# A transformer and two mixing blocks on one core: the second blocks' stages in another order

## The chip, the cores and the metric

The kernel runs on one core of a Trainium2 chip. The metric is the device time of one execution in microseconds (us). Runs are compared by their median.

## The reference, cut to what matters

The input has 256 latent and 256 context tokens of width 1024. Two transformer layers with attention and feed-forward parts come first; the change does not touch them. Then come two "second blocks" on the 256 latent tokens, and the change is in their first part, the mixer:

```python
def second_block(x, ...):
    for l in range(2):
        h = rms_norm(x, g_mix[l])
        aq, ak, av, iq, ik, iw, glu_in, cc_in, sb_in, gate_in = split(h @ w_in[l])
        # qa, ka, qi, ki: norms and rotary products of aq, ak, iq, ik
        y_a = dsa_attention(qa, ka, va, qi, ki, iw) @ w_oa[l]     # 4 heads of 128, the 64 best keys of a query
        u = causal_dwconv(glu_a * sigmoid(glu_b), cb_conv_w[l], cb_conv_b[l])     # 31 taps, 512 channels
        y_b = silu(layer_norm(u, ...)) @ w_ob[l]
        y_c = (gb * causal_dwconv(gc * xc, cc_conv_w[l])) @ w_oc[l]               # 3 taps
        y_d = stick_breaking_attention(sq, sk, sv) @ w_od[l]                      # 4 heads of 128
        gates = sigmoid(gate_in + b_gate[l])                                     # 4 x 1024
        merged = gates[0]*y_a + gates[1]*y_b + gates[2]*y_c + gates[3]*y_d
        x = x + merged @ w_merge[l]
        # feed-forward part with a convolution of 3 taps, unchanged
```

## The kernel before, in words

All matrix products are fp32 products made of three: every weight w is split into w_hi (ACT casts it, `split` at L1219) and w_lo = w - w_hi (DVE subtracts, `split` at L1713), every activation likewise, and `products` (L713) multiplies hi by hi, lo by hi and hi by lo. Weights come in **units** (`Run`, `Unit`, L165 to L185): 256 columns by eight blocks of 128 rows, 1 MB, 48 matmuls of 256 columns on PE. The units of w_oa to w_od have four row blocks, half of all that; ik and iw are smaller still. SP loads unit n when unit n-4 is done. `split_ahead(u)` (L1230, L1723) splits the unit two behind u, so each stage of ACT and DVE carries the splits of what follows. There are three w_hi, four w_lo and three PSUM slots; PE opens a unit (`open_unit`, L703) when w_lo is ready and the slot's user three units earlier has been read.

Nothing is scheduled by a planner. `plan_second` (L393) lists stages and what they count; each engine then walks the list and runs its own function of a stage's kind, in program order, with semaphores between them. So the order within a queue is written out by hand. The stages of a second block's mixer, with the start of each in the profiled execution's first one:

- **glu** (4 units, from 1815), **cc** (4) and **cb** (2): ACT evacuates or applies the sigmoid, DVE multiplies. The 31-tap convolution starts once glu's output `cb_in` is there: channels 256 to 511 on GpSimd (`conv`, L2531: two products and a sum per tap), channels 0 to 255 on DVE (`conv_taps`, L2359: two instructions per tap, chained through `cb_sum`). DVE's 31 taps are laid beside cc and cb (2 per unit), aq and ak (3 per unit), iw (1) and av (3 per unit). GpSimd then waits for DVE's last tap, runs the 3-tap convolution (`cc`, L2559) and writes `oc_hi` and `oc_lo` until 2017.
- **heads** aq, ak (2 units each), iq, ik (`heads`, L889, L1385, L1973): PE, then a copy to `kept` by ACT, squares, sums by PE (L916), rotation by PE (L922), rotary products by DVE (`turned`, L2001), whose first one frees the unit's PSUM. **iw** and **av** follow.
- **select** (L1116, L1551, L2288): PE transposes the index weights, computes eight score products, ACT applies relu, DVE sums into `idx` and finds the 64 best with maximum and replace instructions, 22 turns for both query tiles, with a split after each second turn. The first unit of sq waits for all eight relus.
- **sq** (4), **sv** (2), **gates** 0 (4) on PE, beside DVE's selection.
- **soft** (L1002, L1493, L2137), from 2012.9: selected attention as eight items (head and query tile). DVE waits for the last `oc_lo` before it starts, since `cb_in` shares its place with the branches. PE puts half a unit of gates 1 beside each item (`beside`, L805); they are kept without the sigmoid.
- **stick** (L1138, L1605, L2394), from 2050.2: two pairs of heads; scores, logarithms on ACT, masks on GpSimd (L2582), suffix sums on PE (L1158), exponentials, weighing. The four half units of w_oa are beside it, one after the scores and one after the sums of each pair. DVE multiplies them by their gates straight away (`add_branch`, L1737).
- **layernorm** (L1186, L1646, L2439), from 2083.6, by itself: column sums, squares, Ln and Exp, Silu, split into `ob_hi` and `ob_lo` by DVE.
- **gates** 2, branch ob, **gates** 3, branches oc and od, then **merge** (from 2173.6) and the feed-forward part. The sigmoid of gates 1 is taken at the start of gates 2 (L1664).

`beside` units use two halves of PSUM bank ps[2] in turn; a third one waits until the first is read.

## Time and profile before

| | |
|---|---|
| median of 3 runs | 2998.51 us (2997.86 to 3007.01) |
| profiled execution | 2996.51 us, of which the span of its instructions is 2994.8 us |
| first second block, mixer (1815 to 2173.6) | 358.6 us |
| PE, DVE, ACT, GpSimd (POOL) busy | 94%, 66%, 39%, 17% of the span |
| TensorE clock granted, mean | 0.976 |
| HBM read | 423.5 MB, 142 GB/s |

The rows are read like this. A row of a group names line, engine, operation, what it writes and reads, shapes and count; then busy us and mean ns of one, and the idle time before. In a row of stretches the busy us and counts of PE, PEld (weight loads), DVE, ACT and POOL follow the length, and behind them the granted clock as a share of 2.4 GHz, the DMA engines' busy share and GB/s. In a timeline a bracket holds the idle time before an instruction and what ended it. In the list of waits, "PE ps L718 <- ACT rel L1561" is PE idle before line 718 until ACT's line 1561 had ended.

### The profile page before, as it was taken

The page shows a single profiled execution, that of the slowest core. Times are in us where ns is not written, and L with a number is a line of the kernel's source. Part 1 is how long each engine was busy: PE and PEld are TensorE (multiplying, and loading weights), DVE is VectorE, ACT ScalarE, POOL GpSimd, SP SyncE. Part 2 cuts the span into 40 slices and gives each one's busy share as a digit, 9 for nine tenths or more (in the row PEclk, how much of TensorE's full clock was granted, in tenths as well). Part 3 has the DMA queues.
Part 4 walks back from the last instruction along what each step waited for, and adds up shares of the span by engine and source line. Part 5 has one row for each costly group of instructions (what it writes and reads, how often), then busy time and mean ns, then how long its engine had stood idle before and what let it go on. Part 6 is the DMA issues. An engine that isn't in the chain of part 4 may idle for free.

```text
span 2994.8 us, 43644 instructions
## 1 busy us (share of the span) xinstructions
PE 2818.2 (94%) x18194; PEld 2530.4 (84%) x18194; DVE 1976.3 (66%) x2865; ACT 1168.5 (39%) x1564; POOL 520.8 (17%) x400
## 2 busy tenths in 40 slices
PE   5999999979999999999999999888989997989999
PEld 3888887848888888888868999887989997989999
DVE  3777754485767767465666657975566679756665
ACT  4212154375212252122655334444444444444443
POOL 0200100010100101010000103991000049710000
PEclk8999999999999999999999999999999999999999
DMA  7556532202555545353304666442556663425565
GB/s 249 176 160 192 175 100 85 71 1 85 172 172 182 172 120 180 114 162 124 124 29 115 179 172 172 132 141 86 174 160 180 176 170 106 148 92 183 155 180 144
DMA packets 593171, 427.37 MB, mean 143 GB/s; under 512 B 16848, under 2 KB 571088, under 8 KB 592720
## 3 DMA queue, kind: packets, MB, share of 16 engines
q1 hardware_dynamic: 592976, 424.59, 47.3%
q8 instruction: 144, 2.36, 0.3%
q14 instruction: 51, 0.42, 0.0%
HBM read 423.50 MB, written 1.05 MB: 142 GB/s over the span
## 4 chain that ended last, share of the span: by engine, by line
PE 69%; POOL 12%; DVE 8%; ACT 5%; DMA 3%; issue 3%; SPq 0%; ACTq 0%; DVEq 0%; POOLq 0%
PE ps L718 20%; PE ps L719 20%; PE ps L720 20%; POOL cb_product L2541 5%; DVE w_lo L1720 3%; POOL cb_sum L2547 3%; ACT w_hi L1228 3%; DMA raw<-in_w_in 1%; POOL cc_product L2541 1%; DVE tap_t L2490 1%; PE ps L939 1%; PE ps L938 1%; PE ps L937 1%; PE pm L916 1%; PE ps L1065 1%
## 5 line engine op out<-in xcount | busy, mean ns | idle before, releaser
L718 PE MATMUL ps<-h_hi,w_hi 128*128 128x256 f32 (+1 forms) x3744 | 1200.2, 321 | 60.3 <-DVE h_lo L1844 22.6
L719 PE MATMUL ps<-h_lo,w_hi 128*128 128x256 f32 (+1 forms) x3744 | 1189.6, 318 | 0.0
L720 PE MATMUL ps<-h_hi,w_lo 128*128 128x256 f32 (+1 forms) x3744 | 1188.8, 318 | 0.0
L1720 DVE TENSOR_TENSOR w_lo<-raw,w_hi 128x2048 fp32r<-128x2048 f32 (+2 forms) x376 | 809.9, 2155 | 357.6 <-ACT w_hi L1228 355.2
L718 PEld LDWEIGHTS ps<-h_hi,w_hi 128*128 128x128 f32 x3744 | 727.6, 194 | 114.2 <-issue 34.3
L1228 ACT CAST w_hi<-raw 128x2048 fp32r<-128x2048 f32 (+2 forms) x376 | 631.2, 1679 | 453.8 <-PE ps L720 298.7
L719 PEld LDWEIGHTS ps<-h_lo,w_hi 128*128 128x128 f32 x3744 | 728.0, 194 | 43.5 <-issue 0.2
L720 PEld LDWEIGHTS ps<-h_hi,w_lo 128*128 128x128 f32 x3744 | 727.4, 194 | 43.0
L2514 POOL TENSOR_TENSOR act_lo<-sil,act_hi 128x512 fp32r<-128x512 f32 (+1 forms) x132 | 159.7, 1210 | 1883.4 <-DVE act_hi L1964 1334.7
L718 PE MATMUL ps<-act_hi,w_hi 128*128 128x256 f32 (+1 forms) x1122 | 367.7, 328 | 1.3 <-DVE w_lo L1720 1.2
L719 PE MATMUL ps<-act_lo,w_hi 128*128 128x256 f32 (+1 forms) x1122 | 366.5, 327 | 0.0
L720 PE MATMUL ps<-act_hi,w_lo 128*128 128x256 f32 (+1 forms) x1122 | 366.5, 327 | 0.0
L1792 DVE SCALAR_TENSOR_TENSOR dot_t<-chunk_w,cond_all 128x1024 f32<-128x1024 f32 x256 | 310.4, 1259 | 5.5 <-DMA chunk_w<-in_ada_t 5.5
L1378 ACT ACTIVATE sil<-ps 128x512 f32<-128x512 f32 (+1 forms) x88 | 47.9, 544 | 562.9 <-PE ps L720 562.9
L718 PEld LDWEIGHTS ps<-act_hi,w_hi 128*128 128x128 f32 x1122 | 213.4, 190 | 21.0 <-DVE w_lo L1720 2.3
L719 PEld LDWEIGHTS ps<-act_lo,w_hi 128*128 128x128 f32 x1122 | 213.4, 190 | 18.1
L720 PEld LDWEIGHTS ps<-act_hi,w_lo 128*128 128x128 f32 x1122 | 213.4, 190 | 17.9
L1879 DVE SCALAR_TENSOR_TENSOR xs<-ps,mod_sb,xs 128x256 f32<-128x256 f32 x136 | 60.5, 479 | 160.0 <-PE ps L720 159.9
L2541 POOL TENSOR_SCALAR cb_product<-cb_in,vec_sb 128x256 f32<-128x256 f32 x120 | 162.3, 1362 | 5.9
L1962 DVE TENSOR_TENSOR sil<-sil,ps 128x512 f32<-128x512 f32 (+1 forms) x88 | 54.4, 618 | 144.1 <-ACT sil L1378 144.1
L2547 POOL TENSOR_TENSOR cb_sum<-cb_sum,cb_product 128x512 f32<-128x512 f32 x60 | 99.8, 1664 | 5.0
L937 PE MATMUL ps<-w_hi,h_hi 128*128 128x256 f32 x288 | 82.2, 285 | 5.2 <-DVE rope_t L2010 5.2
(288 smaller groups left out, 2880.4 us busy)
## 6 DMA issues: line engine op xcount, KB each, us to landing
chunk_w<-in_ada_t SPq DMA_DIRECT2D x128, 512.0 KB, 3.4
raw<-in_w_in SPq DMA_DIRECT2D x62, 1024.0 KB, 5.2
raw<-in_ffn_pre_wi SPq DMA_DIRECT2D x88, 512.0 KB, 5.2
raw<-in_ffn_post_wi SPq DMA_DIRECT2D x88, 512.0 KB, 5.1
raw<-in_ffn_pre_wo SPq DMA_DIRECT2D x32, 704.0 KB, 4.6
raw<-in_ffn_post_wo SPq DMA_DIRECT2D x32, 704.0 KB, 4.7
raw<-in_w_ffn_gate SPq DMA_DIRECT2D x44, 512.0 KB, 4.0
raw<-in_w_ffn_up SPq DMA_DIRECT2D x44, 512.0 KB, 5.3
```

The costliest lines, as they stand in the source:

```text
L718: pe.matmul(o, hi, x_hi[:, k, tok], start=k == 0, stop=False)
L719: pe.matmul(o, hi, x_lo[:, k, tok], start=False, stop=False)
L720: return pe.matmul(o, weights(w_lo[u.low], u, k, m * P, P), x_hi[:, k, tok], start=False, stop=k == u.run.kc - 1)
L937: pe.matmul(o, h_hi[:, k, tok], hi, start=k == 0, stop=False)
L1228: nc.scalar.copy(w_hi[u.slot][:, 0:n], whole[:, 0:n]).then_inc(hi_ready, 1)
L1720: nc.vector.tensor_tensor(w_lo[u.low][:, 0:n], whole[:, 0:n], w_hi[u.slot][:, 0:n].bitcast(F32), ALU.subtract).then_inc(lo_ready, 1)
L1792: nc.vector.scalar_tensor_tensor(dot_t[st], chunk_w[n % 2], 1.0, cond_all[:, st, :], ALU.mult, ALU.mult, accum_out=mod_sb[s.layer][:, at_f ...
L1879: last = nc.vector.scalar_tensor_tensor(xs[:, c, tok], o, mod_sb[layer][:, which * KC + c, st:st + 1], xs[:, c, tok], ALU.mult, ALU.add)
L1962: nc.vector.tensor_tensor(sil[:, r, 0:N], sil[:, r, 0:N], ps[u.slot][:, 1, 0:N], ALU.mult).then_inc(S[run.free], 1)
L2514: nc.gpsimd.tensor_tensor(o, whole, hi.bitcast(F32), ALU.subtract).then_inc(S[signal], 1)
L2541: ins = nc.gpsimd.tensor_scalar((product if w else dst)[:, c, :], x, weights_of(c, w), None, ALU.mult)
L2547: nc.gpsimd.tensor_tensor(dst[:, chunks, :], dst[:, chunks, :], product[:, chunks, :], ALU.add).then_inc(S[signal], 1)
```

## The change

Only the mixers of the second blocks change. The same units are loaded and multiplied.

- **Taps.** DVE's 31 taps: 3 per unit beside the last two of glu, 2 per unit beside cc and cb, 1 per unit beside av, 1 per head in soft, 4 and 3 beside the first two gate units of ob. None beside aq, ak, iq, ik and iw. GpSimd no longer waits for DVE's last tap before the 3-tap convolution.
- **Places.** `cb_in` and `cc_product` move out of the branches' place into the buffers of the modulation chunks, which are done by then. The index relus get two tiles, `rel0` and `rel1`. So soft no longer waits for `oc_lo`; stick still does.
- **Select.** The index weights are turned at the end of av. The four score products of a query tile come behind the first and the second sq unit, into bank pm; ACT's relu takes two heads at once. DVE puts a split before each query tile's sums and one after each third turn.
- **Soft.** Four items, a whole head each: masks, maxima and halves over 512 columns, with the oc gates' units beside.
- **Stick.** Eight units beside: two of oa, two of od's gates, two of oa, two of od's gates. PE: scores of both heads, three units, sums, scores of the next pair, a unit, weighing, three units, sums, a unit, weighing.
- **Then** oc, ob's gates, od, ob, merge. Sigmoids of the oc and od gates are taken in four parts beside oc. Layer norm's column sums follow the third gate unit of ob, its squares the fourth; Ln, Exp and Silu run beside od, and GpSimd writes `ob_lo`.

The core of the diff (ACT's and DVE's written-out orders in soft and ACT's in stick are left out; they follow PE's):

```diff
-        tap = 0
-        for st, per in zip([c, *stages[ahead[0] + 1:]], (2, 3, 3, 0, 0, 1, 3)):
-            runs = (c.pair.n + c.run.n) if st is c else st.run.n
-            st.taps = (g, tap, per)
-            tap = min(tap + per * runs, CB_TAPS)
...
-        sel = Stage("select", waits=[("head_done", k.b["head_done"] + 1), ("psum_read_act", v.run.f0 + 2)])
...
-        q = Stage("plain", run=add(Run("sq", 4, KC, 2 * P, cols_of(w, OFF["sb"], 2 * P), "act")), h=h,
-                  waits=[("idx_relu", sel.b["idx_relu"] + nt * HEADS2)])
+        sel = Stage("select", waits=[("head_done", k.b["head_done"] + 1)])
...
+        v.select = (sel, iw_run)
...
+        q = Stage("plain", run=add(Run("sq", 4, KC, 2 * P, cols_of(w, OFF["sb"], 2 * P), "act")), h=h)
+        q.select = sel
...
-        g1 = Stage("beside", run=gates_of(1), i=1, l=l)
-        a = soft(items, P ** -0.5, "av", "oa", nt, [(gates.run.free, gates.run.f0 + 4)], beside=g1)
...
-        first = branch_of(0, "oa", w_oa, "beside")
-        t = Stage("stick", waits=[("s_out", a.b["s_out"] + HEADS2), (g1.run.free, g1.run.f0 + 4)], beside=first)
...
+        oc_gates = Stage("beside", run=gates_of(2), i=2, pos=1, l=l)
+        a = Stage("soft", waits=[(gates.run.free, gates.run.f0 + 4)], beside=each_of(oc_gates))
...
+        oa_first = Stage("beside", run=branch_of(0, w_oa, 0, 2), x="oa", pos=0, l=l).takes(merged=2)
+        od_gates_first = Stage("beside", run=gates_of(3, 0, 2), i=3, pos=2, l=l)
+        oa_last = Stage("beside", run=branch_of(0, w_oa, 2, 2), x="oa", pos=0, l=l).takes(merged=2)
+        od_gates = Stage("beside", run=gates_of(3, 2, 2), i=3, pos=2, l=l)
+        t = Stage("stick", waits=[("s_out", a.b["s_out"] + HEADS2), (oc_gates.run.free, oc_gates.run.f0 + 4)],
+                  beside=[*each_of(oa_first), *each_of(od_gates_first), *each_of(oa_last), *each_of(od_gates)])
...
+        oc = Stage("branch", run=branch_of(2, w_oc), x="oc", pos=1, l=l, late=(oc_gates, od_gates),
+                   waits=[("cc_out", c.b["cc_out"] + 4), (od_gates.run.free, od_gates.run.f0 + 2)]).takes(merged=4, late_gates=4)
+        ob_gates = Stage("gates", run=gates_of(1), i=1, pos=3, l=l, h=h, waits=[(oc.run.free, oc.run.f0 + 4)])
+        od = Stage("branch", run=branch_of(3, w_od), x="od", pos=2, l=l, waits=[("od_out", t.b["od_out"] + HEADS2)]).takes(merged=4)
...
-        Stage("gates", run=gates_of(2), i=2, l=l, waits=[(first.run.free, first.run.f0 + 4)], h=h, late=g1).takes(late_gates=1)
-        second = branch_of(1, "ob", w_ob, waits=[("ob_out", n.b["ob_out"] + 4)])
-        Stage("gates", run=gates_of(3), i=3, l=l, waits=[(second.run.free, second.run.f0 + 4)], h=h)
-        branch_of(2, "oc", w_oc, waits=[("cc_out", c.b["cc_out"] + 4)])
-        br = branch_of(3, "od", w_od, waits=[("od_out", t.b["od_out"] + HEADS2)])
+        ob_gates.centre = od.centre = n
+        br = Stage("branch", run=branch_of(1, w_ob), x="ob", pos=3, l=l, ready=("ob_out", n.b["ob_out"])).takes(merged=4)
+        tap = 0
+        for st, per, at_most in ((g, 3, 6), (c, 2, 12), (v, 1, 2), (a, 1, 4), (ob_gates, 4, CB_TAPS)):
+            st.taps = (g, tap, per, min(tap + at_most, CB_TAPS))
+            tap = st.taps[3]
+        assert tap == CB_TAPS
...
-    cb_in, cb_sum = over("cb_in", 16, (4, SEQ + CB_TAPS - 1)), over("cb_sum", 28, (4, SEQ))
+    cb_in, cb_sum = place("cb_in", (4, SEQ + CB_TAPS - 1), chunk_at), over("cb_sum", 28, (4, SEQ))
...
-    cb_product, cc_product = over("cb_product", 36, (4, SEQ)), over("cc_product", 16, (4, SEQ))
+    cb_product, cc_product = over("cb_product", 36, (4, SEQ)), place("cc_product", (4, SEQ), chunk_at + 5 * 1024)
...
+                    if i >= 2:
+                        pe.wait_ge(S["s_out"], b["s_out"] + i - 1)
+                    for k in range(2):
+                        last = pe.matmul(pm[:, i % 2, 0:SEQ], values_of("av", k, slice(i * P, (i + 1) * P)),
+                                         attn_t[:, i % 2, k * SEQ:(k + 1) * SEQ], start=k == 0, stop=k == 1)
+                    last.then_inc(S["s_chunk"], 1)
+                scores(0)
+                scores(1)
+                whole_beside(s, 0)
+                turn(0)
+                scores(2)
+                beside(s, 1, 0)
+                weigh(0)
+                beside(s, 1, 1)
+                turn(1)
+                scores(3)
+                beside(s, 2, 0)
+                weigh(1)
+                beside(s, 2, 1)
+                turn(2)
+                beside(s, 3, 0)
+                weigh(2)
+                turn(3)
+                beside(s, 3, 1)
+                weigh(3)
...
+            def turn_weights(s, iw_run):
+                pe.wait_ge(S[iw_run.free], iw_run.f0 + 1)
...
+            def index_scores(s, q):
+                b = s.b
+                waits_of(pe, s)
+                if q:
+                    pe.wait_ge(S["idx_relu"], b["idx_relu"] + 2)
+                else:
+                    pe.wait_ge(S["iw_kept"], b["iw_kept"] + 1)
...
+            def plain(s):
+                for j in range(s.run.n):
+                    dense(Unit(s.run, j), SEQ, (h_hi, h_lo))
+                    if j < 2:
+                        index_scores(s.select, j)
...
             def gates(s):
-                sweep(pe, s.run, lambda u: dense(u, SEQ, (h_hi, h_lo)))
+                for j in range(s.run.n):
+                    dense(Unit(s.run, j), SEQ, (h_hi, h_lo))
+                    if s.centre is not None and j == 2:
+                        column_sums(s.centre)
+                    if s.centre is not None and j == 3:
+                        column_squares(s.centre)
...
+                whole_beside(s, 0)
+                whole_beside(s, 1)
+                whole_beside(s, 2)
+                sums(0)
+                sums(1)
+                scores(2)
+                scores(3)
+                whole_beside(s, 3)
+                weigh(0)
+                weigh(1)
+                whole_beside(s, 4)
+                whole_beside(s, 5)
+                whole_beside(s, 6)
+                sums(2)
+                sums(3)
+                whole_beside(s, 7)
+                weigh(2)
+                weigh(3)
...
+            def late(st, half):
+                at_c = st.pos % 2 * KC + half * KC // 2
+                act.wait_ge(S[st.run.free], st.run.f0 + st.run.n)
+                g = gates_sb[:, at_c:at_c + KC // 2, :]
+                nc.scalar.activation(g, g, ACT.Sigmoid).then_inc(S["late_gates"], 1)
...
+                    if s.late:
+                        late(s.late[j // 2], j % 2)
                     split_ahead(Unit(s.run, j))
+                    if s.centre is not None and j == 0:
+                        column_deviations(s.centre)
+                    if s.centre is not None and j == 2:
+                        activated(s.centre)
...
+                    if u.j == 2:
+                        dve.wait_ge(S["conv_pad"], s.b["conv_pad"] + 1)
+                        dve.wait_ge(S[s.run.free], u.out)
+                    if u.j >= 2:
+                        conv_taps(s, u.j - 2)
...
-                def beside(j):
-                    u = Unit(s.beside.run, j)
-                    split_ahead(u)
-                    add_branch(s.beside, u, beside_bank[j % 2])
...
+                ahead(0)
+                add(0)
+                softplus(0)
+                softplus(1)
+                add(1)
+                ahead(1)
+                argument(0)
+                argument(1)
+                ahead(2)
+                negative(2)
+                negative(3)
+                ahead(3)
+                softplus(2)
+                softplus(3)
+                keep(0)
+                keep(1)
+                ahead(4)
+                add(4)
+                add(5)
+                ahead(5)
+                ahead(6)
+                argument(2)
+                argument(3)
+                ahead(7)
+                keep(2)
+                keep(3)
...
+            def gates(s):
+                if s.behind is not None:
+                    return
+                for j in range(s.run.n):
+                    split_ahead(Unit(s.run, j))
+                    conv_taps(s, j)
+                    if j == 3:
+                        centred(s.centre)
...
+                    if s.pos in (1, 2):
+                        dve.wait_ge(S["late_gates"], s.late_from + u.j // 2 + 1)
                     add_branch(s, u, ps[u.slot][:, :, 0:SEQ])
+                    if s.centre is not None and u.j == 1:
+                        divided(s.centre)
...
-                pool.wait_ge(S["conv_first"], s.conv.b["conv_first"] + 2 * CB_TAPS)
...
+            def layernorm(s):
+                for c in range(4):
+                    pool.wait_ge(S["ln_hi"], s.b["ln_hi"] + c + 1)
+                    hi, lo = (t[:, c, :] for t in branch["ob"])
+                    rest(lo, cb_sum[:, c, :], hi, "ob_out")
```

## Rows read from the trace of the kernel before

**Rows 1.** The page, section 1: busy us, share of the span, instructions
```profile
PE 2818.2 (94%) x18194; PEld 2530.4 (84%) x18194; DVE 1976.3 (66%) x2865; ACT 1168.5 (39%) x1564; POOL 520.8 (17%) x400
```
**Rows 2.** Stretches of the first second block (last row: eight of the other): start:end, length, busy
```profile
1815.00:1887.00 72.00, 71.98 (x578) 71.97 (x579) 54.87 (x64) 31.98 (x32) 42.85 (x30) 0.96 0.56 161
1887.00:1951.50 64.50, 49.02 (x346) 45.23 (x344) 63.23 (x79) 25.17 (x39) 61.85 (x45) 0.91 0.36 107
1951.50:2012.90 61.40, 60.46 (x481) 60.26 (x481) 45.02 (x73) 26.25 (x26) 59.33 (x42) 0.95 0.49 155
2012.90:2050.20 37.30, 32.95 (x256) 31.04 (x256) 22.78 (x56) 16.66 (x37) 3.78 (x6) 1.00 0.27 85
2050.20:2083.60 33.40, 26.90 (x152) 23.55 (x152) 20.61 (x28) 14.54 (x20) 7.55 (x8) 0.90 0.37 115
2083.60:2125.10 41.50, 38.79 (x304) 37.61 (x304) 20.14 (x29) 22.73 (x29) 0.00 (x0) 1.00 0.41 131
2125.10:2173.60 48.50, 46.34 (x384) 46.14 (x385) 30.21 (x32) 18.71 (x24) 0.00 (x0) 1.00 0.57 183
...
sum 588.90, PE 545.28 PEld 532.03 DVE 407.14 ACT 249.94 POOL 191.57; mean PE 68.16 PEld 66.50 DVE 50.89 ACT 31.24 POOL 23.95
```
**Rows 3.** PE's waits, 1887 to 2200: us in total, times, longest
```profile
PE ps L718 <- ACT rel L1561: 7.8, 1, 7.8
PE ps L1158 <- POOL z L2582: 5.2, 2, 4.2
PE ps L718 <- DVE rope_t L2010: 3.7, 1, 3.7
PE ps L718 <- DVE w_lo L1720: 3.4, 3, 2.1
PE ps L937 <- DVE rope_t L2010: 2.6, 1, 2.6
...
PE pm L1194 <- ACT ln_t L1650: 1.4, 1, 1.4
PE ps L1147 <- DVE oa_lo L1757: 1.0, 1, 1.0
PE pm L1190 <- DVE od_lo L1757: 1.0, 1, 1.0
PE ps L1012 <- ACT gates_sb L1241: 0.9, 1, 0.9
PE pm L1120 <- ACT xs L1436: 0.8, 1, 0.8
```
**Rows 4.** Short stretches of the same view: granted clock is PEclk, the third number from the end
```profile
1888.30:1894.40 6.10, 6.10 (x51) 6.08 (x50) 6.10 (x9) 2.94 (x3) 5.92 (x5) 1.00 0.38 80
1907.30:1915.80 8.50, 8.50 (x49) 8.50 (x50) 8.47 (x12) 2.53 (x5) 8.18 (x6) 0.66 0.00 0
1951.50:1960.10 8.60, 8.59 (x50) 8.59 (x51) 8.46 (x17) 1.75 (x1) 8.24 (x7) 0.65 0.00 0
...
2057.80:2060.30 2.50, 2.50 (x13) 2.22 (x13) 0.69 (x1) 0.14 (x1) 0.59 (x2) 1.00 0.70 249
2072.30:2077.10 4.80, 4.80 (x13) 3.88 (x13) 0.69 (x1) 0.36 (x1) 1.12 (x2) 0.52 0.05 17
```
**Rows 5.** DVE's groups, 1887 to 1951.5: busy, mean ns
```profile
L2372 DVE SCALAR_TENSOR_TENSOR cb_sum<-cb_in,vec_sb,cb_sum 128x256 f32<-128x256 f32 x33 | 23.0, 758 | 0.0
```
**Rows 6.** DVE's timeline, 1864 to 1867: start, us, instructions
```profile
1864.68 2.27 DVE L2372 SCALAR_TENSOR_TENSOR cb_sum<-cb_in,vec_sb,cb_sum 128x256 f32<-128x256 f32 x4
```
**Rows 7.** Timelines: GpSimd's products and last oc_lo, DVE's first mask
```profile
1843.90 3.75 POOL L2541 TENSOR_SCALAR cb_product<-cb_in,vec_sb 128x256 f32<-128x256 f32 x2
...
1854.58 1.99 POOL L2541 TENSOR_SCALAR cb_product<-cb_in,vec_sb 128x256 f32<-128x256 f32 x2
...
2016.23 0.74 POOL L2514 TENSOR_TENSOR oc_lo<-cc_sum,oc_hi 128x256 fp32r<-128x256 f32 x1
...
2017.00 0.42 DVE L2150 SCALAR_TENSOR_TENSOR logits<-ps,sel_mask 128x256 f32<-128x256 f32 x1 [1.90 <-POOL oc_lo L2514]
```
**Rows 8.** The chain that ended last, at 2115.5: start, us, what
```profile
2115.50 5.29 DMA raw<-in_w_in
```
**Rows 9.** DVE's groups, 1842 to 2017: busy, mean ns, idle before
```profile
L1720 DVE TENSOR_TENSOR w_lo<-raw,w_hi 128x2048 fp32r<-128x2048 f32 (+2 forms) x26 | 62.2, 2394 | 21.0 <-ACT w_hi L1228 20.8
```

More of the change, by code:

```diff
@@ L1034, in weigh @@
[L1034 to L1047 removed]
+                    if i >= 2:
+                        pe.wait_ge(S["s_out"], b["s_out"] + i - 1)
@@ new lines, in gate @@
+                def gate(n):
+                    gate_out(*s.beside[n], beside_bank[n % 2], ACT.Identity)
+                exponentials(0)
+                exponentials(1)
+                split_ahead(s.beside[0][1])
+                gate(0)
+                copied(0)
+                exponentials(2)
+                split_ahead(s.beside[1][1])
+                gate(1)
+                copied(1)
+                exponentials(3)
+                split_ahead(s.beside[2][1])
+                gate(2)
@@ L1522, in pairs @@
+                copied(2)
+                split_ahead(s.beside[3][1])
+                copied(3)
+                gate(3)
             def pairs(s):
@@ L1646, in layernorm @@
-            def layernorm(s):
-                b = s.b
+                ahead(0)
+                exp(0)
+                exp(1)
+                log(0)
+                log(1)
+                ahead(1)
+                act.wait_ge(S[oa[0].run.free], oa[0].out)
+                gate(2)
+                ahead(2)
+                kept(2)
+                kept(3)
+                weights_(0)
+                weights_(1)
+                ahead(3)
+                exp(2)
+                exp(3)
+                log(2)
@@ L2200, in soft @@
-                for step in (masked, maximum, negative):
-                    step(0)
-                for i in range(n):
-                    for following, step in ((masked, total), (maximum, reciprocal), (negative, normed)):
-                        if i + 1 < n:
-                            following(i + 1)
-                        step(i)
-                    if s.beside and i % 2 == 0:
-                        split_ahead(Unit(s.beside.run, i // 2))
-                    if i >= 2 and (i - 2) % s.per == s.per - 1:
-                        chunk_out((i - 2) // s.per)
@@ new lines, in soft @@
+                dve.wait_ge(S["sel_mask"], b["sel_mask"])
+                masked(0)
+                maximum(0)
+                negative(0)
+                masked(1)
+                maximum(1)
+                negative(1)
+                reciprocal(0)
+                normed(0)
+                split_ahead(s.beside[0][1])
+                conv_taps(s, 0)
+                masked(2)
+                maximum(2)
+                negative(2)
+                reciprocal(1)
+                normed(1)
@@ new lines, in soft @@
+                split_ahead(s.beside[1][1])
+                conv_taps(s, 1)
+                chunk_out(0)
+                masked(3)
+                maximum(3)
+                negative(3)
+                reciprocal(2)
+                normed(2)
+                split_ahead(s.beside[2][1])
+                conv_taps(s, 2)
+                chunk_out(1)
+                reciprocal(3)
+                normed(3)
+                split_ahead(s.beside[3][1])
+                conv_taps(s, 3)
+                chunk_out(2)
@@ L2311, in wait_last @@
                         dve.wait_ge(S["top_steps"], last[q])
-                behind = [Unit(run, j) for run in s.runs for j in range(run.n)]
                 turns = [0]
```

409 lines of the change are left out of this document (174 added, 235 removed).

## The prediction

> **What bounds the kernel now.** I read the page first, for the engine that sets the end. PE is busy 2818 of 2994.8 us [rows 1], so only time in which PE idles or runs slowly can be won. Next the two second blocks were cut at their stage borders and each stretch read for its length against PE's busy time [rows 2]. Glu and outer convolution (1815 to 1887) have no idle time. From there to the merge (2173.6) it is 15.5 us in heads, values and index scores, 0.9 beside the top-k, 4.35 in the selected attention, 6.5 in stick-breaking, 2.7 in layer norm and gates, 2.2 in the last branches: 32.1 us. The other second block is alike (588.9 us for eight stretches that take 590.0 here). The list of PE's waits gives the causes [rows 3]: 7.8 us before the first sq unit, behind the index relu; 3.7 and 2.6 for DVE's rotary product, which frees PSUM; 5.2 for GpSimd's mask in stick-breaking; 3.4 for w_lo at three transitions to large units. Last the granted clock beside those waits [rows 4]: the stretch of an ordinary unit takes 6.1 us at 1.00 (2.4 GHz), those behind the 3.7 and 7.8 us waits 8.5 and 8.6 at about 0.65, in part at 1.2 GHz. The stick-breaking sums take 2.5 us in the first pair and 4.8 in the second, after 4.2 idle, at 0.52. That costs 2.4, 2.8 and 2.3: 7.5 us per block.
>
> **Heads, values and select: -15.0 idle, -5.2 clock.** PE waits for the rotary product because DVE is full: 63.2 busy in 64.5 us [rows 2], 23.0 of it in 33 taps [rows 5]. The change moves the taps: six instructions each beside two glu units, four beside each cc and cb unit as before, two instructions beside each av unit, two beside each selected head, and eight and six beside the first two gate units of ob. Of the 33 in this stretch only the four beside av stay. At the 0.76 us mean the other 29 free 22 us, leaving DVE 41 in 64. A key unit then costs DVE a split of 2.3, two cosines 1.5, sines 0.8, sum 1.0 and product 1.05, thus 6.7, under PE's 7.5 from one key unit to the next (6.1 and two small products of 1.0 that overlap a little). So 3.7, 2.6 and 0.6 go. Where iq, ik and iw follow each other with little PE work, av finds its PSUM bank free within about a microsecond of needing it; I leave 0.5. The index scores move into the sq units, one whole PE unit ahead of each relu: the 7.8 and the 0.8 before the turned weights go. Their matmuls stay. ACT's relus become four of 0.6 instead of eight, between splits that have 2 us of slack. The top-k starts a unit later relative to sq, but it is 22 turns of 0.75 to 1.5 us, some 21 us, beside ten splits of 2.3 in 60 us of PE work; it still ends behind the last split and 1.5 us after it, as now. The 0.9 before the scores stays.
>
> **Taps beside glu: 0.** Twelve instructions at 0.57 (four took 2.27 [rows 6]) are 7 us; DVE is busy 54.9 of 72 us there [rows 2]. Without that cover it would cost PE 7 us per block. The convolution on GpSimd starts 2.2 us later.
>
> **Selected attention: -3.35.** The same PE work, by heads: two score matmuls, a gate unit of 5.8 us, four transposes, two weighings. DVE's turn for a head (mask 0.7, maximum 0.7, negative and reciprocal 0.3, two scalings 0.7, split 2.3, taps 1.1, halves 0.85) is 6.7 against PE's 7.8. The longest circle, negative to exponentials 1.2, ACT split 1.9, DVE split, taps, halves and next mask, is 9.0, but it turns only twice and starts a gate unit ahead; its splits are small from the third head on. I find no wait but the last 1.0 for oa_lo [rows 3], which the next stage still needs. DVE no longer waits for oc here: now it goes on only at 2017.00, when GpSimd's last oc_lo has ended at 2016.97 [rows 7].
>
> **Stick-breaking: -6.5, clock -2.3.** PE gets two gate units more per pair: 11.5 us between scores and sums where 3.1 stand now. The chain from scores to mask is 7.6 us (2050.2 to 2057.8), with a large split inside 9.9, so it fits; the same for the sums to the weights, behind a gate or half unit. Beside units 2 to 7 need their bank read by the unit two before: DVE's product or ACT's gate follows each in 1 to 2 us, and a unit of 2.9 to 5.8 lies between.
>
> **Gates, layer norm, branches: -0.9.** Layer norm's 1.4 and 1.0 go, hidden behind gate unit 4 and the od branch. Two stalls stay or come. oc's four half units (11.5 us) before a large one: its load is issued after the first, lands in 5.3 [rows 8] and takes 1.9 and 2.3 to split, 9.5 against 8.6 of PE: 0.9 (now 1.1). The last taps: DVE's split for the third gate unit, eight taps, a split and six taps end about 0.9 us after PE has done that unit, where the column sums wait for them. The 2.1 before the merge stays. The silu chain needs about 12 us to the last ob_lo; od gives 11.5 and the order by k of ob's first unit 2 more.
>
> **The sum** per block is 15.0 + 3.35 + 6.5 + 0.9 + 7.5 = 33.3; for two, less 0.6 because the second block's slow sums cost less, 66. No queue order of this length goes through without new small waits; those of 0.4 to 0.8 us in the list of waits are their size, and I take two per block at 0.75, with ends of 0 and 6 us per block. So 63 us off the profiled execution's 2996.5, 2933.5. The median of the runs shown stands 2.0 above it; predicted 2935.
>
> **GpSimd, and a rule against the change.** Stick-breaking on DVE waits for cc_out, and PE comes to it 24 us earlier. The product pair takes 1.99 us alone and 3.75 where a split of DVE runs beside it [rows 7]: 1.75 us per split. GpSimd's work from 1842.7 to 2017.0 holds 26 splits [rows 9]. In the new order four splits less of PE time go by before the same PE place, so some two to four more fall into GpSimd's work: 2017 + 2.2 + 4 is 2023, and DVE needs it at 2050.2 - 24 + 2 = 2028. Five us of slack: 0.
> The Trainium skill (SBUF — State Buffer, Who interferes with whom) says that a DVE instruction with two SBUF inputs and a GpSimd one that reads SBUF share a read interface as an exclusive lock: the later one fully blocks. By that a split would cost its whole 2.3 us rather than 1.75, and this rule speaks against the tighter order. The rows show three quarters of it.
>
> **Rivals.** *A: the gaps close* as above. 0.70, 2923 to 2948.
> *B: GpSimd late.* If each of some 28 splits costs 2.3 instead of 1.75, GpSimd ends 15 us later, at 2038, 10 after DVE's need; 1 to 2 of it is hidden by the first beside unit. 8 us in each block: 2951. For it: DVE waits for GpSimd even today. Against: the rate measured in the same kernel, and some 34 taps that no longer run beside it in keys and values. 0.12. This is where the page's rule would lead.
> *C: new waits take the place of old ones*, in the written-out orders of ACT and DVE, one of about 3 us with half a clock loss of 1.2 in each of four stages: 17 us per block, 2968. For it: each engine is in order, and the 9.0 us circle. 0.11.
> *D: slower.* The twelve beside units of a block (eight large) hang on banks that ACT or DVE must read before PE goes on. If each stood still as the second pair's sums do now, 4.2 idle and 2.3 clock, 24 units would cost 156 us: 3089. It decides from 63/24 = 2.6 us per unit on. Against: today's beside units never wait for their bank. 0.04.
> *E: not what it says.* If the stream of weights set the pace, PE would wait for it elsewhere: about 2990. DMA is busy 0.26 to 0.63 and FFN units hold 5.8 us. 0.03.
>
> **Numbers.** A, B and C are faster: 0.93; E is within 0.3% (9 us, about what a measurement of this kernel tells from no change): 0.03; D slower: 0.04. Range 2923 (no new waits, a few us of matmuls saved by fewer starts) to 2962, which takes in A and B and part of C.
>
> **What would show it.** Right: PE's wait for the relu gone from its list and none above 2 us between heads and merge but the merge's 2.1; granted clock near 1.00 there; heads to merge near 253 us instead of 286.6; taps on DVE in the glu stretch; GpSimd's last oc_lo some us before DVE's first negative of z. Wrong: a wait of DVE for oc_lo (B); PE waits for attn, z or gates above 2 us (C, D); column sums waiting long for cb_sum.

## The result: 2930.2 us, and the profile after

The changed kernel takes 2930.22 us (median of 4 runs, 2929.32 to 2934.05) against 2998.53 of the kernel before (4 runs, 2997.86 to 3007.01): ratio 0.9772, 95% interval 0.9759 to 0.9785. The profiled execution took 2930.85 us with a span of 2929.1, 65.7 less than before. That is faster, by 68.3 us in the medians, where 63 were forecast. Of the six executions of e2 below one took 3637.74 us at a granted clock of 0.712; the median given there is of all six, that of the other five is 2925.68.

The page of the changed kernel, section 1, against [rows 1]:

```profile
PE 2791.6 (95%) x18162; PEld 2512.1 (86%) x18162; DVE 1955.8 (67%) x2817; ACT 1176.6 (40%) x1564; POOL 535.0 (18%) x408
```

PE is busy 26.6 us less with nearly the same instructions, and idle 39.1 us less (176.6 before, 137.5 after). Inside the two mixers PE is busy 18.6 us less and idle 43.5 us less: the first is mostly clock, the second waits, and both belong to the forecast. Outside them, where both kernels are the same, it is busy 8.0 less and idle 4.4 more. Where the mixers' part went shows in the stretches of the first second block, cut at the new stage borders (start:end, length, then PE, PEld, DVE, ACT, POOL busy; the third number from the end is the granted clock). They stand against [rows 2]:

```profile
1812.20:1884.00 71.80, 71.79 (x580) 71.72 (x581) 56.01 (x72) 32.59 (x33) 42.23 (x27) 0.97 0.58 162
1884.00:1927.50 43.50, 42.68 (x327) 40.39 (x325) 36.03 (x43) 21.31 (x28) 41.77 (x29) 1.00 0.48 134
1927.50:1988.00 60.50, 60.44 (x498) 59.20 (x497) 51.80 (x82) 28.16 (x30) 58.32 (x38) 1.00 0.58 175
1988.00:2025.10 37.10, 32.37 (x240) 30.62 (x240) 28.43 (x45) 17.10 (x35) 29.50 (x29) 1.00 0.30 88
2025.10:2071.70 46.60, 46.58 (x345) 45.15 (x345) 26.74 (x30) 23.87 (x33) 6.51 (x8) 1.00 0.38 125
2071.70:2084.60 12.90, 11.79 (x98) 11.56 (x96) 8.52 (x11) 8.59 (x9) 0.00 (x0) 1.00 0.82 258
2084.60:2111.00 26.40, 26.38 (x208) 25.99 (x209) 19.00 (x28) 12.56 (x18) 0.00 (x0) 1.00 0.36 112
2111.00:2138.70 27.70, 23.75 (x194) 23.28 (x192) 20.33 (x26) 15.83 (x23) 4.14 (x4) 1.00 0.71 229
sum 326.50, PE 315.76 PEld 307.90 DVE 246.85 ACT 160.00 POOL 182.45; mean PE 39.47 PEld 38.49 DVE 30.86 ACT 20.00 POOL 22.81
```

The rows are: glu and outer convolution; heads and values; sq to the first gates; selected heads; stick-breaking; the oc branch; the gates of ob with the layer norm's matmuls; the od and ob branches. From the first glu unit to the first merge unit it is 326.5 us instead of 358.6, and 327.7 instead of 357.7 in the other block: 62.1 together. The other 3.6 of the 65.7 lie outside the mixers, 2.8 of them before the first one, where both kernels are the same (more on that at the end).

PE's waits from the heads to the merge (us in total, times, longest), against [rows 3]:

```profile
PE ps L715 <- DVE w_lo L1806: 5.1, 3, 3.1
PE ps L1024 <- DVE attn L2258: 2.9, 2, 2.2
PE ps L1173 <- DVE oa_lo L1843: 1.0, 1, 1.0
PE ps L1014 <- ACT gates_sb L1275: 0.9, 1, 0.9
PE ps L939 <- DVE rope_t L2096: 0.8, 1, 0.8
PE ps L715 <- DVE h_lo L2187: 0.4, 1, 0.4
```

The 7.8 for the relu, the 5.2 for the mask, the 3.7 and 2.6 for the rotary product and the layer norm's 1.4 are gone. The waits for attn (VectorE's scaled weights in the selected heads) are 2.9 us and are not new as such: the kernel before has waits of that name, in a row that [rows 3] leaves out.

```profile
PE ps L1020 <- DVE attn L2190: 2.3, 2, 1.5
```

The waits for w_lo grew from 3.4 to 5.1. The question for the experiments is which part of the change took which wait away, and what the two largest that are left, for attn and for w_lo before the merge, hang on. Below, "mixers" means the time from the first glu unit to the first merge unit, read from each profile, because it is free of what varies elsewhere.

### The profile page after: what moved, and what is told of

Its sections match the earlier page's. It is cut to its first block, busy times and chain, and to the rows that moved or that the text cites. A ratio compares the mean times of both kernels' runs of the same rounds, so it can differ in the third digit from the quotient of the medians.

```text
span 2929.1 us, 43506 instructions
## 1 busy us (share of the span) xinstructions
PE 2791.6 (95%) x18162; PEld 2512.1 (86%) x18162; DVE 1955.8 (67%) x2817; ACT 1176.6 (40%) x1564; POOL 535.0 (18%) x408
## 4 chain that ended last, share of the span: by engine, by line
PE 81%; DVE 10%; ACT 5%; DMA 2%; issue 2%; SPq 0%; ACTq 0%; DVEq 0%
PE ps L715 23%; PE ps L716 23%; PE ps L717 23%; DVE w_lo L1806 4%; ACT w_hi L1262 3%; PE ps L939 1%; PE ps L940 1%; PE ps L941 1%; PE ps L815 1%; PE ps L816 1%; PE ps L817 1%; PE pm L918 1%; DMA raw<-in_w_in 1%; DVE tap_t L2606 1%; PE ps L1073 1%
## 5 line engine op out<-in xcount | busy, mean ns | idle before, releaser
L715 PE MATMUL ps<-h_hi,w_hi 128*128 128x256 f32 (+1 forms) x3616 | 1156.8, 320 | 40.9 <-DVE h_lo L1930 24.1
L716 PE MATMUL ps<-h_lo,w_hi 128*128 128x256 f32 (+1 forms) x3616 | 1146.6, 317 | 0.0
L717 PE MATMUL ps<-h_hi,w_lo 128*128 128x256 f32 (+1 forms) x3616 | 1146.1, 317 | 0.0
L715 PEld LDWEIGHTS ps<-h_hi,w_hi 128*128 128x128 f32 x3616 | 695.8, 192 | 92.9 <-issue 27.7
L716 PEld LDWEIGHTS ps<-h_lo,w_hi 128*128 128x128 f32 x3616 | 696.0, 192 | 43.3 <-issue 0.2
L717 PEld LDWEIGHTS ps<-h_hi,w_lo 128*128 128x128 f32 x3616 | 695.8, 192 | 43.2
L2657 POOL TENSOR_SCALAR cb_product<-cb_in,vec_sb 128x256 f32<-128x256 f32 x120 | 176.9, 1484 | 5.9
L2663 POOL TENSOR_TENSOR cb_sum<-cb_sum,cb_product 128x512 f32<-128x512 f32 x60 | 106.3, 1771 | 5.0
```

Of the source, the lines that this page charges most:

```text
L715: pe.matmul(o, hi, x_hi[:, k, tok], start=k == 0, stop=False)
L716: pe.matmul(o, hi, x_lo[:, k, tok], start=False, stop=False)
L717: return pe.matmul(o, weights(w_lo[u.low], u, k, m * P, P), x_hi[:, k, tok], start=False, stop=k == u.run.kc - 1)
L2657: ins = nc.gpsimd.tensor_scalar((product if w else dst)[:, c, :], x, weights_of(c, w), None, ALU.mult)
L2663: nc.gpsimd.tensor_tensor(dst[:, chunks, :], dst[:, chunks, :], product[:, chunks, :], ALU.add).then_inc(S[signal], 1)
```

## Experiments: one part undone at a time

**e1: the taps back on the head units.**

```diff
-        for st, per, at_most in ((g, 3, 6), (c, 2, 12), (v, 1, 2), (a, 1, 4), (ob_gates, 4, CB_TAPS)):
+        for st, per, at_most in ((c, 2, 12), (aq_stage, 3, 6), (ak_stage, 3, 6), (iw_stage, 1, 1), (v, 3, CB_TAPS)):
```

> The changed kernel with the VectorE taps where they stood before (two a unit beside cc and cb, three a unit beside the head units, one beside iw, three beside each av unit; none beside glu, the selected heads and the gates of ob). Theory (VectorE is full beside the head units, and its late rotary product holds PSUM): TensorE's waits for rope_t of 3.7 and 2.6 us come back with the half clock behind them, 6.9 - 0.5 idle and 2.4 of clock per block, while the two waits for attn in the selected heads (2.9 us) go: +5.9 per block, 2942 us, ratio to before 0.981. Rival (the gain came from the new order of values and index scores, the taps' places are indifferent): no wait for rope_t over 1 us and the attn waits gone, 2924.

Measured: 2944.77 us, ratio 0.9822 (0.9807 to 0.9837). The mixers are 335.8 and 334.7 us, 9.2 and 7.0 longer than in the changed kernel (5.9 forecast). The waits, 1884 to 2160, and below them three short stretches with their clock: before the long wait, the unit behind it, and the first av unit behind the 2.8.

```profile
PE ps L715 <- DVE rope_t L2096: 4.5, 2, 4.0
PE ps L939 <- DVE rope_t L2096: 2.8, 1, 2.8
PE ps L1118 <- DVE rope_t L2096: 1.0, 1, 1.0
```

```profile
1891.50:1899.60 8.10, 7.71 (x56) 7.18 (x56) 8.03 (x9) 3.36 (x5) 7.74 (x6) 1.00 0.08 12
1904.00:1911.10 7.10, 7.10 (x49) 7.07 (x48) 7.07 (x10) 2.53 (x5) 6.74 (x6) 0.76 0.00 0
1924.90:1931.50 6.60, 6.60 (x43) 6.60 (x44) 6.38 (x8) 2.68 (x3) 6.33 (x5) 0.75 0.08 26
```

VectorE is busy 8.03 of 8.10 us ahead of the wait, and the clock behind each wait is part at 2.4 and part at 1.2 GHz. The waits for attn are gone from this list. So the taps beside the heads cost PE 8.3 us of idle and, by these two stretches, 1.7 of clock each, the taps beside the selected heads 2.9 of idle in this block: the rival, that their place is indifferent, is out.

**e4: the index scores ahead of sq, unparted.** PE issues both groups before the first sq unit, ScalarE's four relus stand before its sq work.

```diff
+                for q in range(2):
+                    index_scores(s.select, q)
                 for j in range(s.run.n):
                     dense(Unit(s.run, j), SEQ, (h_hi, h_lo))
-                    if j < 2:
-                        index_scores(s.select, j)
```

> The index scores of both query tiles stand ahead of the first sq unit again, but keep their own PSUM tile and their four relus. Theory (what cost 7.8 us before was that the sq units had to wait for banks that eight relus still read; the scores themselves wait for little): about 0.8 us for the turned weights and 1.4 for two relus between the two score groups, 2.2 per block and no half clock: 2935. Rival (the place between the sq units is what hides them): the 7.8 us wait and 2.8 of clock come back, 10 per block, 2951.

Measured: 2931.56 us, ratio 0.9778 (0.9763 to 0.9792); the mixers 1.8 and 0.3 us longer. Two waits stand in the place of the old 7.8, in a stretch with clock 1.00:

```profile
PE pm L1142 <- ACT rel L1599: 1.3, 1, 1.3
PE pm L1142 <- ACT iw_sb L1638: 0.6, 1, 0.6
```

The place between the sq units is worth 1.9 us of idle per block, not the 8.6 (7.8 and 0.8) for which the prediction had named it the reason.

**e9 and e10: what the 7.8 us were made of.** In e9 PE also waits for all four relus before the first sq unit, as the shared banks of the kernel before forced it to. In e10, besides, the taps are placed as in e1 and one relu buffer serves both tiles (VectorE's split moves behind the sums, so that it can't wait for a ScalarE split that stands behind the relus).

```diff
+                pe.wait_ge(S["idx_relu"], s.select.b["idx_relu"] + 4)
...
+                    if q:
+                        act.wait_ge(S["idx_sum"], b["idx_sum"] + 2 * pair + 2)
-                    nc.scalar.activation(rels[q][:, 2 * pair:2 * pair + 2, :], pm[:, :, pair * SEQ:(pair + 1) * SEQ], ACT.Relu,
+                    nc.scalar.activation(rels[0][:, 2 * pair:2 * pair + 2, :], pm[:, :, pair * SEQ:(pair + 1) * SEQ], ACT.Relu,
```

> As e4, and TensorE also waits for all four relus before the first sq unit, as if the scores still stood in the banks of the sq units. Theory (the shared banks by themselves cost one relu pair): 1.2 us on top of e4's 1.9 per block, no half clock: 2934. Rival (the banks were the reason of the old 7.8 us wait): a wait of over 4 us with half clock, 2945 or more.

> As e9, with the taps on the head and value units as in e1, and one relu buffer for both query tiles, so that the second tile's relus wait for VectorE's sums of the first (as before). Theory (the old 7.8 us were VectorE again: the relus waited for its sums, and those stood behind six taps of 4.1 us): in the profile of e8 VectorE ends those taps 1.1 us after the second scores; with 2.3 us of sums and the last relu TensorE waits about 4.6 us before the first sq unit, and the half clock comes back: +6.5 per block over e1 and e4, 2960. Rival (taps and buffer don't meet, the wait stays at e9's 1.2 us): 2950.

Measured: e9 2930.06 us, ratio 0.9772 (0.9756 to 0.9788), wait 1.2 us as expected; the mixers are 2.0 and 0.2 longer than in the changed kernel and not the 3.1 expected, since the waits for attn fell from 2.9 to 0.5 in the same profile. e10 2965.74 us, ratio 0.9889 (0.9875 to 0.9904); the mixers are 344.5 and 345.0. Over e1 and e4 together that is 7.0 and 9.9 per block where 6.5 were expected. VectorE's timeline in e10 (start, us), then the wait, then the clock of the unit behind it:

```profile
1938.73 4.12 DVE L2466 SCALAR_TENSOR_TENSOR cb_sum<-cb_in,vec_sb,cb_sum 128x256 f32<-128x256 f32 x6
1942.77 0.47 DVE L2386 SCALAR_TENSOR_TENSOR idx<-rel,iw_sb,con_sb 128x256 f32<-128x256 f32 x1
```

```profile
PE ps L715 <- ACT rel L1602: 5.7, 1, 5.7
```

```profile
1946.40:1953.00 6.60, 6.54 (x42) 6.54 (x43) 4.63 (x4) 1.80 (x2) 6.28 (x5) 0.74 0.00 0
```

The relus of the second tile wait for sums, the sums stand behind six taps. The list names ScalarE as the releaser, but the time was VectorE's: with its taps elsewhere and two relu buffers (e9) the same banks cost 1.2 us. The taps alone and the one buffer alone were not tried, so the runs show the two together. That the 7.8 us of the kernel before were made in the same way shows in its own trace, ScalarE first, then VectorE:

```profile
1941.72 1.21 ACT L1561 ACTIVATE rel<-ps 128x256 f32<-128x256 f32 x4 [0.46 <-PE ps L1128]
1948.54 0.38 ACT L1561 ACTIVATE rel<-ps 128x256 f32<-128x256 f32 x1 [5.60 <-DVE idx L2297]
```

```profile
1943.93 4.12 DVE L2372 SCALAR_TENSOR_TENSOR cb_sum<-cb_in,vec_sb,cb_sum 128x256 f32<-128x256 f32 x6
1947.97 0.47 DVE L2297 SCALAR_TENSOR_TENSOR idx<-rel,iw_sb,con_sb 128x256 f32<-128x256 f32 x1
```

The first tile's relus are done at 1942.93, the sums that they feed start at 1947.97, behind a split and six taps, and the second tile's relus wait 5.60 us for the first of them. By these rows the taps are 4.1 us of the 7.8.

**e6: the stick-breaking sums after one beside unit** in the first pair instead of three.

```diff
                 whole_beside(s, 0)
-                whole_beside(s, 1)
-                whole_beside(s, 2)
                 sums(0)
                 sums(1)
+                whole_beside(s, 1)
+                whole_beside(s, 2)
```

> The sums of the first stick-breaking pair stand after one beside unit instead of three, the other two units follow them; same work. Theory: the mask of that pair ends about 4.4 us after TensorE has done the one unit; TensorE idles that long and the clock falls behind it as in the kernel before (2.3 us there): +6.5 per block, 2943. Rival 1: the idle comes without the clock loss: +4.4 per block, 2939. Rival 2: the chain of ScalarE and VectorE is quicker when TensorE asks for it early, so the wait is under 2 us: 2933 or less.

Measured: 2945.14 us, ratio 0.9824 (0.9809 to 0.9838); the mixers 6.2 and 6.0 us longer, against 6.5. The wait, and the stretches of the wait, of the sums behind it and of the next units:

```profile
PE ps L1184 <- POOL z L2704: 4.5, 1, 4.5
```

```profile
2030.90:2035.30 4.40, 0.00 (x0) 0.00 (x0) 3.77 (x4) 3.43 (x5) 1.01 (x2) 1.00 0.37 119
2035.30:2038.90 3.60, 3.55 (x9) 2.90 (x10) 0.00 (x0) 0.00 (x0) 0.56 (x1) 0.53 0.00 0
2039.00:2050.20 11.20, 11.20 (x87) 10.88 (x86) 4.17 (x4) 1.60 (x3) 1.22 (x2) 1.00 0.21 52
```

After 4.4 us of idle the short sums run at 0.53, nearly all at 1.2 GHz, and the large units behind them at 2.4 again. So the clock costs 3.6 x (1 - 0.53) = 1.7 us here (2.3 forecast for the slow sums of [rows 4]). The mixers' 6.2 is 4.5 and 1.7, but the waits for attn are 0.8 us shorter in this profile, so that about 0.8 of busy time is not accounted for. Rivals 1 and 2 are out.

**e8: e1, e4 and e6 together, and both layer-norm sums after the fourth gate unit.** Beside the edits above:

```diff
-                    if s.centre is not None and j == 2:
-                        column_sums(s.centre)
                     if s.centre is not None and j == 3:
+                        column_sums(s.centre)
                         column_squares(s.centre)
```

> The three edits of this call together, and both sums of the layer norm after the fourth gate unit of ob (alone worth about 1.5 us per block). Theory (the terms lie in different stretches and add up): 12 + 5 + 13 + 3 us on top of 2930, 2963. Rival (an idle engine in one stretch gives the others time, so the terms overlap): under 2950. Rival (waits near each other feed the half clock and so more than add up): over 2975.

Measured: 2970.39 us, ratio 0.991 (0.9894 to 0.9927). The mixers are 18.7 and 19.8 us longer per block. e1, e4 and e6 alone add up to 17.2 and 13.3; the layer norm's share in this profile is 2.2 in the first block (from the oc branch to the merge 69.3 us against 67.1), where 1.5 was expected; 1.4 of it is the old wait for ln_t, which is back in the list.

In the first block the parts add up (17.2 and 2.2 against 18.7). In the other they fall short: 13.3 and 2.0 against 19.8, and most of the 4.5 that are over is busy time of PE (6.6 us more than in the changed kernel, against 1.9 for the three parts together), so clock: the stretches at half the clock behind the 2.8 for rope_t and behind the wait for z last 6.8 and 6.9 us, where they last 3.4 in e1 and in e6. The theory said 33 for both, 38.5 were measured in the mixers, and the median lies between it and the second rival (over 2975): that the waits feed the half clock is true in one block. Left between e8 and the kernel before are 27 us; e10 shows where some 17 of them lie (the relu buffer with the taps). The other 10 were not located. What soft gained by not waiting for oc_lo, and what its four whole heads and the second pair of stick-breaking gave, was never undone.

## Experiments: the two waits that are left

These three ran beside the changed kernel itself.

> The changed kernel itself, as the base for the three kernels beside it: 2930, ratio to before 0.977.

Measured: 2932.71 us, ratio 0.978 (0.9767 to 0.9794).

**e2: the four taps beside the selected heads move into stick-breaking.**

```diff
-(a, 1, 4), (ob_gates, 4, CB_TAPS)
+(t, 1, 4), (ob_gates, 4, CB_TAPS)
...
                 add(1)
                 ahead(1)
+                conv_taps(s, 0)
                 argument(0)
```

The other three stand behind softplus(3), ahead(6) and argument(3).

> The four VectorE taps beside the selected heads move into the stick-breaking stage, where VectorE is busy 27 of 47 us. Theory (the two waits for attn, 2.2 and 0.7 us a block, come from taps that take up to 1.75 us each beside GpSimd's sums and stand on the way to the next head's mask): the waits go, nothing new in stick-breaking: -2.9 per block, 2924.5. Rival 1 (the circle of split, exponentials and mask is too long even without taps): the longer wait stays above 1 us: 2928. Rival 2 (the taps delay the sums' use in stick-breaking, a wait of about 1 us appears there): no gain, 2930.

Measured: 2926.43 us, ratio 0.9762 (0.9749 to 0.9775). The mixers are 323.1 and 323.6 us, 3.6 less each than in the run beside it (326.7, 327.2). The list of PE's waits from 1884 to 2160 in e2 has the other five rows of the changed kernel's list, with the same numbers, and no row for attn: its waits are gone and none came in stick-breaking. Of the 3.6 us half is idle time and half busy time (317.1 to 315.3 us in the first block), since in the run beside it the one wait for attn, of 2.2 us in each block, has a stretch at 1.2 GHz behind it:

```profile
2016.80:2020.20 3.40, 3.40 (x18) 3.40 (x18) 3.17 (x4) 2.37 (x5) 3.18 (x5) 0.50 0.68 240
```

Why four taps did so much shows in the changed kernel's timelines, VectorE's first, then GpSimd's at the same time:

```profile
2000.86 0.91 DVE L2243 TENSOR_SCALAR stats<-stats 128x2 f32<-128x2 f32 x1
...
2007.12 3.49 DVE L2463 SCALAR_TENSOR_TENSOR cb_sum<-cb_in,vec_sb,cb_sum 128x256 f32<-128x256 f32 x2
...
2012.76 0.17 DVE L2243 TENSOR_SCALAR stats<-stats 128x2 f32<-128x2 f32 x1
```

```profile
2005.59 3.85 POOL L2663 TENSOR_TENSOR cc_sum<-cc_sum,cc_product 128x1024 f32<-128x1024 f32 x1
```

Two taps took 3.49 us beside GpSimd's sum. From one negative (2000.86) to the next (2012.76) it is 11.9 us; in e2, without the taps, it is 9.5 (1998.53 to 2008.04).

**e3: in the last branch ScalarE splits before it rounds.**

```diff
-                    if s.next is not None:
-                        merged_hi(s.next, j)
+                    if s.next is not None and j:
+                        merged_hi(s.next, j - 1)
+                if s.next is not None:
+                    merged_hi(s.next, s.run.n - 1)
```

> In the last branch ScalarE makes each unit's split before the rounding of the merged chunks that it waits for. Theory (the splits for ob's last unit and for the first merge unit stand behind a rounding that waits for VectorE's sum): the 0.9 us wait of ob's last unit goes; merge's first load is issued when ob's first unit is done (2125.8 in the profile of the changed kernel), lands 5.7 later and takes 1.9 and 2.3 to split, against 2134.8 for the end of ob: 1.0 instead of 3.1 is left. -2.9 per block, 2924.5. Rival (VectorE's order is what holds the split, or the load): the merge wait stays above 2.5 us and only 0.9 to 1.3 per block go, 2928.

Measured: 2926.35 us, ratio 0.9759 (0.9743 to 0.9774). The mixers are 322.9 and 322.5 us, 3.8 and 4.7 less. ScalarE in the changed kernel, then in e3:

```profile
2129.47 0.71 ACT L1756 CAST h_hi<-spare 128x256 fp32r<-128x256 f32 x2 [4.50 <-DVE spare L1835]
2130.09 1.04 ACT L1262 CAST w_hi<-raw 128x1024 fp32r<-128x1024 f32 x1
2133.81 0.71 ACT L1756 CAST h_hi<-spare 128x256 fp32r<-128x256 f32 x2 [2.69 <-DVE spare L1835]
2134.43 1.90 ACT L1262 CAST w_hi<-raw 128x2048 fp32r<-128x2048 f32 x1
```

```profile
2124.79 1.05 ACT L1262 CAST w_hi<-raw 128x1024 fp32r<-128x1024 f32 x1 [1.25 <-DMA raw<-in_w_ob]
...
2129.38 1.91 ACT L1262 CAST w_hi<-raw 128x2048 fp32r<-128x2048 f32 x1 [0.62 <-DMA raw<-in_w_merge]
```

Each split now starts when its load has landed. PE's wait for w_lo at ob's last unit is gone, the one at the merge fell from 3.06 to 0.62. Rival out: it was ScalarE's written-out order. The 2.1 us of the kernel before, which the prediction let stand as given, had the same order:

```profile
2168.70 0.71 ACT L1676 CAST h_hi<-spare 128x256 fp32r<-128x256 f32 x2 [2.68 <-DVE spare L1749]
2169.32 1.90 ACT L1228 CAST w_hi<-raw 128x2048 fp32r<-128x2048 f32 x1
```

The load for this split was issued at 2162.90 and had landed at 2167.97, 1.35 us before the split. So at most 1.35 of the 2.1 were this order (in the changed kernel it is 3.7: landed at 2130.74, split at 2134.43); no run tried it on the kernel before.

**e7: e2 and e3 together.**

> Both edits together. They lie in different stretches, so they should add up: -5.8 per block, 2919, under both kernels. If the waits only moved on: 2924 or more.

Measured: 2917.6 us, ratio 0.9732 (0.9719 to 0.9745), the mixers 319.5 and 320.0 us. That is 7.2 per block and 15.1 us under the changed kernel's run beside it, where 11.6 were expected; the two add up in the mixers (14.4 against 7.2 and 8.5). This version beats both kernels.

## Why the prediction was right, step by step

Right in its main line: rival A held, the time came out 5 us under the forecast, within the range. The mixers gave 62.1 us of the 63 forecast; the rest of the 68.3 lies where the two kernels are the same. One of its signs for a wrong forecast, named for rivals C and D, appeared all the same: a wait for attn above 2 us (2.17). The wait at the merge was 3.1 us where 2.1 was to stay. From the heads to the merge it is 254.7 us, where about 253 were forecast. Set against the steps, for the first block (idle of PE from the rows above and [rows 2]). The row of the selected heads above starts at 1988.0 and so takes in the 0.9 us before the scores, which [rows 2] counts to the stretch before; with the border as there it is

```profile
1988.90:2025.10 36.20, 32.33 (x240) 30.59 (x240) 28.14 (x44) 16.22 (x33) 28.68 (x28) 1.00 0.31 91
```

| step | forecast | measured |
|---|---|---|
| heads, values, select, gates of oa: idle | -15.0 | -14.7 (16.4 to 1.8) |
| selected heads: idle | -3.35 | -0.5 (4.35 to 3.87) |
| stick-breaking: idle | -6.5 | -6.5 (6.50 to 0.02) |
| gates, layer norm, branches: idle | -0.9 | +0.2 (4.87 to 5.08) |
| clock (PE busy) | -7.5 | -10.7 (326.4 to 315.8) |
| allowance for new waits | +1.5 | in the rows above |
| sum | -31.8 | -32.1 |

- **Heads, values and select.** As forecast, and e1, e9 and e10 show the mechanism: VectorE's taps. One reason was put in the wrong place: the prediction took the 7.8 us as the price of where the index scores stood. Interleaving is worth 1.9; the rest came back only with the taps and the single relu buffer (5.7 in e10 against 1.2 in e9). 0.8 for av's rotary wait, 0.5 forecast.
- **Selected heads: the step that failed.** The circle was put at 9.0 us with taps of 1.1, and said to turn only twice without a wait. It measured 11.9, since two taps took 3.49 beside GpSimd, and PE waited 2.17 and 0.74 us. The term was 0 for a wait that was 2.9, and e2 takes it away. The kernel before waited 1.49 and 0.77 us for attn, without a tap in this stretch, the first time just after VectorE's own wait for oc_lo [rows 7]; the prediction did not name these waits and took them to go. The price was to be had before: the taps of [rows 5] take a mean of 0.76 us in a busy stretch against 0.57 in [rows 6].
- **Stick-breaking.** Exact in its idle time: no wait in 46.6 us but for the 1.0 for oa_lo ahead of it, and e6 brings back 4.5 of idle and 1.7 of clock for one pair.
- **Gates, layer norm, branches.** The 0.9 before the column sums didn't come. In VectorE's timeline

```profile
2099.03 2.46 DVE L2463 SCALAR_TENSOR_TENSOR cb_sum<-cb_in,vec_sb,cb_sum 128x256 f32<-128x256 f32 x6
```

 a tap takes 0.41 us with GpSimd idle (2.46 for six; it was 0.57 in [rows 6]), and the last ends at 2101.49, ahead of the sums at 2102.00. The stall at ob's first gate was 1.14 against 0.9. But where 2.1 was left before the merge, 0.9 came at ob's last unit and 3.06 at the merge: ScalarE's roundings, whose place in its queue the prediction had not followed (e3).
- **Clock.** All stretches after glu read 1.00 in this block. Of the 10.7 us that PE is less busy, 7.5 were the slow stretches of [rows 4]. Of the rest 1.3 is not steady: in the repeat of the same kernel PE is busy 317.1 us here, not 315.8, since 3.4 us behind its wait for attn are at the half clock. In the other block of the changed kernel PE is 7.9 us less busy than before, and there too the clock fell behind the same 2.17 us wait:

```profile
2574.00:2577.40 3.40, 3.40 (x18) 3.40 (x17) 3.26 (x4) 2.26 (x5) 3.20 (x4) 0.51 0.67 231
```

 After one such wait of the changed kernel it fell, after the other it did not; these rows don't show what decides.
- **GpSimd (rival B).** It wasn't late. Its last oc_lo and VectorE's first negative of stick-breaking:

```profile
2017.98 0.78 POOL L2630 TENSOR_TENSOR oc_lo<-cc_sum,oc_hi 128x256 fp32r<-128x256 f32 x1
```

```profile
2026.99 1.48 DVE L2493 SCALAR_TENSOR_TENSOR z<-z 128x512 f32<-128x512 f32 x2 [1.93 <-ACT z L1655]
```

 8.2 us of slack where 5 were forecast. GpSimd hurt all the same, in a way that the prediction had not priced: not by being late, but by slowing VectorE's taps.
- **Rival C** came true in two of four stages, the selected heads (2.9 us, 0.6 of it more than before, and in the other block a wait of 2.2 with its clock loss) and the last branch (1.8 more than before). e7 wins back 7.2 us per block there, waits of the kernel before among them. **D**: no beside unit waited for its bank. **E**: no new wait for the stream of weights appeared; the one at ob's first gate is 1.14 where oc's was 1.1.

So the total was right in part by luck, because errors cancelled: 2.9 us less than forecast was won in the selected heads, 1.1 less at the end and 0.3 less in the heads, against 3.2 more of busy time and the 1.5 of allowance.

## What to carry to other kernels

When an engine in order is full, its lateness shows under other names: here 7.8 us stood to ScalarE's relus, and 4.1 of them were VectorE's convolution taps. Follow a wait back through each queue until an engine that never idles, and move the work that has no due time (taps) out of that stretch. When the order is written out by hand, put a step that waits for a late result (a rounding) behind a step that waits only for a load (a split); and price filler at what it takes beside its neighbour, not alone.

## What was not expected of the hardware

- A VectorE tap (two SBUF inputs, 128x256) lasted 0.47 us with GpSimd idle (one every 0.41, as they overlap) and up to 2.61 beside it. Duration min/median/max in ns of the changed kernel's taps, 1990 to 2112:

```profile
L2463 DVE SCALAR_TENSOR_TENSOR cb_sum<-cb_in,vec_sb,cb_sum x22: 474/476/2608, 1998.4 to 2101.0; 128x256 f32<-128x256 f32 x22
```

 The longest is the one issued at 2007.12, while GpSimd's sum ran from 2005.59 to 2009.44: 2.3 us of that sum were left, and 0.4 of its own makes 2.7. The Trainium skill (SBUF — State Buffer, Who interferes with whom) says that the later of two such instructions waits the earlier one out in full; this row agrees. The prediction found only three quarters of a split on GpSimd; if a GpSimd instruction is issued in the middle of a split, it has only the rest of it to wait. No run tested that reading, and not every row fits it:

```profile
1842.81 4.60 POOL L2657 TENSOR_SCALAR cb_product<-cb_in,vec_sb 128x256 f32<-128x256 f32 x2
1842.90 2.28 DVE L1806 TENSOR_TENSOR w_lo<-raw,w_hi 128x2048 fp32r<-128x2048 f32 x1
```

 Here GpSimd's pair starts 0.09 us before VectorE's split, yet the split takes its usual 2.28 us and the pair 4.60, where it takes 1.99 alone. Spans of GpSimd are rough at this size, so it stays open who blocks whom.
- Where the mixers begin varies between profiles of kernels that are the same up to there: 1808.6 us in e10, 1812.2 in the changed kernel, 1814.6 in its repeat, 1815.0 in the kernel before. In the first 1800 us PE's busy time is the same to about 3 us in these profiles, but in e10 it gets through a few more instructions, at a granted clock of 0.99 against 0.98 (this row is of e10; the repeat has x9575 and 0.98 in 1714.74 us):

```profile
0.00:1800.00 1800.00, 1716.37 (x9623) 1458.22 (x9624) 1147.66 (x1717) 652.89 (x915) 139.44 (x100) 0.99 0.46 139
```

 So 2.8 of the 65.7 us between the two spans, and differences of some us between any two medians here, are not the change's. The lengths of the mixers vary by about 1 us and are the better measure of a part.
